# Block two of a transformer kernel: fill matmuls and a paired start at each layer's entry, and one weight panel more ahead in the group norm

## What is computed

```python
h = _rmsnorm(x, norm_g) * (1.0 + scale[:, None, :]) + shift[:, None, :]
proj = h @ w_in
(q, k, v, g_att, qi, ki, wi, z, xbc, dt_raw, gl_att, gl_ssd) = _split_cols(proj, IN_SIZES)
...
y_att = (o_att * jax.nn.silu(g_att)) @ w_branch_a
...
y = y.reshape(B, L, D_SSM) * jax.nn.silu(z.astype(jnp.float32))
y = y.reshape(B, L, N_GROUPS, D_SSM // N_GROUPS)
y = y * lax.rsqrt(jnp.mean(y * y, axis=-1, keepdims=True) + EPS)
y = (y.reshape(B, L, D_SSM) * ssm_norm_g.astype(jnp.float32)).astype(x.dtype)
y_ssd = y @ w_branch_s
merged = jax.nn.sigmoid(gl_att) * y_att + jax.nn.sigmoid(gl_ssd) * y_ssd
return x + gate[:, None, :] * (merged @ w_out)
```

## Time and profile before

| what | us |
|---|---|
| median of 3 runs | 2490.84 (2490.64 to 2492.44) |
| the profiled execution, its time | 2492.25 |
| the profiled execution, its span | 2490.5 |
| TensorE busy in it | 2397.2 |
| VectorE busy | 1421.7 |
| ScalarE busy | 1020.8 |
| POOL busy | 273.9 |
| mean granted TensorE clock, share of full | 0.98 |

### The profile page before, as it was taken

How to read it: one execution, slowest core, us unless ns; L and a number is a source line. 1 busy time by engine, 2 the same in 40 slices (tenths; PEclk the granted TensorE clock), 3 DMA queues, 4 the chain that set the end, 5 groups by cost and what they waited for, 6 DMA issues and landing times.

```text
span 2490.5 us, 31846 instructions
## 1 busy us (share of the span) xinstructions
PE 2397.2 (96%) x11996; PEld 1933.0 (78%) x11996; DVE 1421.7 (57%) x2366; ACT 1020.8 (41%) x1732; POOL 273.9 (11%) x260
## 2 busy tenths in 40 slices
PE   8998899999999999999999989999999899999998
PEld 7876788888887888788888856778788677677886
DVE  3545665655655666566456459947533478665333
ACT  3655564322334444443233334444322344444223
POOL 0000011000000000100000236302000133111001
PEclk9999799999999999999999989999999999999999
DMA  5211002333332111134334212201222221102321
GB/s 193 94 51 43 1 18 93 140 141 127 142 129 87 67 52 60 60 110 152 137 112 159 96 57 68 68 26 43 85 95 94 74 71 65 43 27 76 102 93 51
DMA packets 58038, 211.75 MB, mean 85 GB/s; under 512 B 6432, under 2 KB 6560, under 8 KB 57888
## 3 DMA queue, kind: packets, MB, share of 16 engines
q1 hardware_dynamic: 57456, 208.86, 24.1%
q10 hardware_dynamic: 432, 0.85, 0.1%
HBM read 207.60 MB, written 2.10 MB: 84 GB/s over the span
## 4 chain that ended last, share of the span: by engine, by line
PE 83%; DVE 7%; issue 5%; ACT 4%; POOL 1%; DMA 0%; SPq 0%; ACTq 0%; DVEq 0%; POOLq 0%
PE bank L458 75%; PE last_bank L458 5%; PE bank L468 3%; DVE arena L1105 1%; DVE arena L2190 1%; DVE arena L2192 1%; ACT wparts L545 1%; DVE small L796 1%; ACT arena L784 1%; DVE wparts L549 0%; POOL rstd L604 0%; DVE hT L707 0%; DVE hv L699 0%; DMA ring<-weights_dram 0%; ACT arena L2098 0%
## 5 line engine op out<-in xcount | busy, mean ns | idle before, releaser
L458 PE MATMUL bank<-hT,wparts 128*128 128x512 f32 x5568 | 1353.5, 399 | 16.7 <-DVE hT L707 6.6
L458 PEld LDWEIGHTS bank<-hT,wparts 128*128 128x128 f32 x5568 | 1043.4, 190 | 259.2 <-issue 23.1
L549 DVE TENSOR_TENSOR wparts<-ring,wparts 128x1024 fp32r<-128x1024 f32 x290 | 366.9, 1265 | 433.1 <-ACT wparts L545 432.8
L458 PE MATMUL bank<-arena_r,wparts 128*128 128x512 f32 x2400 | 566.1, 396 | 0.0
L458 PEld LDWEIGHTS bank<-arena_r,wparts 128*128 128x128 f32 x2400 | 450.0, 188 | 108.5 <-DVE arena_r L579 0.3
L545 ACT ACTIVATE wparts<-ring 128x1024 fp32r<-128x1024 f32 x332 | 348.4, 1050 | 163.7 <-PE bank L458 135.7
L784 ACT ACTIVATE arena<-bank,small 128x128 f32<-128x128 f32 (+3 forms) x192 | 101.1, 527 | 142.0 <-DVE small L796 140.5
L468 PE MATMUL bank<-cf_sb,arena 128*128 128x128 f32 (+1 forms) x816 | 134.6, 283 | 17.7 <-DMA cf_sb<-cf_dram 4.7
L458 PE MATMUL last_bank<-arena 128*128 128x64 f32 x992 | 139.6, 279 | 8.0 <-DVE arena L819 3.8
L458 PEld LDWEIGHTS last_bank<-arena 128*128 128x128 f32 x992 | 131.3, 201 | 15.9 <-issue 8.5
L796 DVE TENSOR_REDUCE small<-bank 128x1 f32<-128x128 f32 (+3 forms) x192 | 93.4, 487 | 58.6 <-PE bank L458 56.7
(11 more groups left out here) (273 smaller groups left out, 2113.1 us busy)
## 6 DMA issues: line engine op xcount, KB each, us to landing
ring<-weights_dram SPq DMA_DIRECT2D x388, 512.0 KB, 3.3
arena<-x_dram SPq DMA_DIRECT2D x4, 512.0 KB, 5.7
out_dram<-arena SPq DMA_DIRECT2D x4, 512.0 KB, 4.0
rot<-rot_dram SPq DMA_DIRECT2D x1, 512.0 KB, 10.5
rot<-rot_dram ACTq DMA_DIRECT2D x1, 512.0 KB, 2.9
cf_sb<-cf_dram SPq DMA_DIRECT2D x1, 416.0 KB, 8.8
cb_sb<-cb_dram SPq DMA_DIRECT2D x1, 264.0 KB, 9.8
vecs<-vec_dram ACTq DMA_DIRECT2D x1, 258.5 KB, 5.8
```

Source lines behind the costliest of these rows:

```text
L458: i = pe.matmul(*args, **kw)
L549: eng.tensor_tensor(wparts[:, slot, 1, :, :], ring[:, p % RAW, :, :], wparts[:, slot, 0, :, :].bitcast(F32), ALU.subtract)\
```

## The change

- New `pe_pair`: takes two banks and, for each k, waits for h once and runs the three matmuls of panel one and the three of panel two. `project` uses it for its first two items when `busy` is given; those are qi 0 and qi 1 in both layers. The rope of item 0 is then issued directly behind the pair, and the rope of item 1 after the first 9 matmuls of kki.
- New `pe_busy`: so many bf16 matmuls of 512 columns (identity by a constant) into the bank that was just taken; the real product then overwrites it. 15 ahead of the tokens `xn`, 7 ahead of the spread `L0h`, 9 ahead of the pair in layer 0; 12 ahead of the tokens, 5 ahead of the spread, 12 ahead of the pair in layer 1. Where fills stand, the bank is taken before the wait.
- `AHEAD[4]` is `gls` instead of `gla`.

```diff
+        def pe_pair(pe, keys, rhs, ready, busy=0):
+            taken = [banks.take(pe, key) for key in keys]
+            pe_busy(pe, taken[0], busy)
+            first = tile_no[0]
+            for k in range(KD):
+                pe.wait_ge(*ready(k))
+                for m, (key, bank) in enumerate(zip(keys, taken)):
+                    tile_no[0] = first + KD * m + k
+                    (hi, lo), ends = tile_of(pe)
+                    last = k == KD - 1
+                    mm(pe, bank[:, :], lhsT=hi, rhs=rhs[:, 0, k, :], start=(k == 0), stop=False)
+                    mm(pe, bank[:, :], lhsT=hi, rhs=rhs[:, 1, k, :], start=False, stop=False)
+                    mm(pe, bank[:, :], lhsT=lo, rhs=rhs[:, 0, k, :], start=False, stop=last,
+                       done=key if last else None, ends=ends)
+            for m, key in enumerate(keys):
+                banks.panel_of[key] = first // KD + m
+
+        def pe_busy(pe, bank, n):
+            for _ in range(n):
+                mm(pe, bank[:, :], lhsT=identb, rhs=cstb("cmp")[:, 0:SEQ], start=True, stop=True)
...
-        def pe_by_token(pe, key, sums, weight, last):
+        def pe_by_token(pe, key, sums, weight, last, busy=0):
 
             pe.wait_ge(*pool_made["means"])
-            pe.wait_ge(*pool_made[last])
-            bank = banks.take(pe, (key, "ms"))
+            if busy:
+                bank = banks.take(pe, (key, "ms"))
+                pe_busy(pe, bank, busy)
+                pe.wait_ge(*pool_made[last])
+            else:
+                pe.wait_ge(*pool_made[last])
+                bank = banks.take(pe, (key, "ms"))
...
-        def pe_all_partitions(pe, key, diagonal, pool=ALL_BANKS):
-            pe.wait_ge(*dve_made[key, "diagonal"])
-            bank = banks.take(pe, (key, "rep"), pool)
+        def pe_all_partitions(pe, key, diagonal, pool=ALL_BANKS, busy=0):
+            if busy:
+                bank = banks.take(pe, (key, "rep"), pool)
+                pe_busy(pe, bank, busy)
+                pe.wait_ge(*dve_made[key, "diagonal"])
+            else:
+                pe.wait_ge(*dve_made[key, "diagonal"])
+                bank = banks.take(pe, (key, "rep"), pool)
...
-                    pe_by_token(pe, key, sums, 0, (key, "sum", KD - 1))
-                    pe_all_partitions(pe, key, sums)
+                    pe_by_token(pe, key, sums, 0, (key, "sum", KD - 1), 12)
+                    pe_all_partitions(pe, key, sums, busy=5)
...
-                    linear = pe_linear_steps(pe, it["key"], it["n"], hT, KD, ready if i == 0 else None, pool)
+                    if busy is not None and i < 2:
+                        if i == 0:
+                            pe_pair(pe, [(two["key"], two["n"]) for two in items[:2]], hT, ready, busy)
+                        linear = iter(())
+                    else:
+                        linear = pe_linear_steps(pe, it["key"], it["n"], hT, KD, ready if i == 0 else None, pool)
...
-            pe_by_token(pe, "xn", s1, 0, ("xn", "sum", KD - 1))
+            pe_by_token(pe, "xn", s1, 0, ("xn", "sum", KD - 1), 15)
             pe_by_token(pe, "xs", s2, 0, ("xs", "sum", KD - 1))
-            pe_all_partitions(pe, "L0h", s2)
+            pe_all_partitions(pe, "L0h", s2, busy=7)
             pe_all_partitions(pe, "xn", s1)
...
-            then(project(items, h_at(hk), rtmp, vt, ROPE32))
+            then(project(items, h_at(hk), rtmp, vt, ROPE32, busy=12 if l else 9))
...
-            AHEAD = {0: "ya", 4: "gla"}
+            AHEAD = {0: "ya", 4: "gls"}
```

More of the change, by code:

```diff
@@ L892, in lo_of, with project @@
             return lambda k: dve_made[(key, k), "lo"]
-        def project(items, ready, rtmp, vt, table=None, vt_free=None, pool=ALL_BANKS, norm=None, first=False, summed=False):
+        def project(items, ready, rtmp, vt, table=None, vt_free=None, pool=ALL_BANKS, norm=None, first=False, summed=False, busy=None):
             made = act_made if norm is None else dve_made
```

## The result

The changed kernel takes 2475.07 us (median; 2474.76 to 2478.57), before it was 2491.39 in the same session: ratio 0.9938, 95% interval 0.9926 to 0.9951. That is 16 us, 0.62%. The forecast was 2475.0, with 2470 to 2482 as range. The profiled execution of the changed kernel took 2478.57, its span is 2476.7.

A forecast was written before the change was run, and what follows sets the result against it. TensorE, busy for 96% of the span and holding 83% of the chain that ended last, bounds the kernel. Gains of 5.5 + 4.2 + 2.8 + 1.3 + 2.8 = 16.6 from 2492.25 give 2475.7; forecast 2475.0, range 2470 to 2482.

The forecast's parts named there:

- the 5.5 taken: Layer 0's entry: gain chosen between 3.0 (clock falls) and 6.2 (clock full throughout), near the upper end.
- Price of a fill: All fills: a bf16 matmul of 512 columns takes 0.23 us at full clock, 0.43 at the low clock.
- Layer 0 with the clock full: Layer 0's entry: faster tokens (-1.4), faster spreads (-1.5) and the paired panels gain 6.2 us in all.
- Rival A: The clock falls in layer 0's entry in most executions, which gains 3.0, not 5.5: about 2477.7 us; chance 0.20.
- the spreads keep 1.5: Layer 0's entry if the clock falls: the spreads stay 1.5 us slower, part of why only 3.0 is left.
- Layer 1: Layer 1's entry: fills halve the spread (-1.0) and the pair shortens the projection, -4.2 us, ends 3.2 and 5.0.
- Group norm: Merges: converting the second gls panel early removes TensorE's wait, -2.8 us per layer; layer 0's clock stays up, -1.3 more.
- rival B: Another wait replaces the group norm's, giving back up to 2.3 us in each layer: about 2480 us; chance 0.09.
- Rival C: Both entries: fills overrun their holes and the pair runs at the low clock, slower overall: about 2504 us; chance 0.02.
- Rival D: The pairing buys nothing, TensorE being on VectorE's pace already; the second panel's 5.5 stays: about 2483 us; chance 0.05.
- Sum: Whole kernel: 5.5 + 4.2 + 2.8 + 1.3 + 2.8 = 16.6 us gained, giving 2475.7 from the profiled 2492.25.

The follow-up runs named there:

- double_fills: The changed kernel with every group of fills doubled (30, 14, 18; 24, 10, 24): 2482.74 us, ratio 0.9968 to the kernel before.
- full_again: The changed kernel unaltered, run again in a later session beside variants: 2472.88 us, ratio 0.9926 to the kernel before.
- dve_last_sum: The changed kernel, with VectorE instead of POOL adding the last of eight sums of squares, and shorter fills (12, 5, 9; 9, 5, 12): 2478.22 us, repeated 2474.23.
- fewer_fills: The changed kernel with every group of fills cut by half (8, 4, 5; 6, 3, 6): 2478.75 us, ratio 0.9953 to the kernel before.
- gn_only: The kernel before with only the group norm's key changed (gls for gla), both entries as before: 2485.22 us against 2490.73, ratio 0.998.
- fills_only: The changed kernel without the pair and without the group norm's key, third fills ahead of the first panel: 2486.87 us, ratio 0.9988.

## Why the prediction was right

The time came out at the forecast, and most terms did too. But the forecast assumed that the clock would seldom fall in layer 0's entry, and it fell in three profiles of four; that layer 0 still gained the 5.5 taken is partly luck, as the second and third points show.

- *Price of a fill*, taken as 0.23: 14 and 7 at full clock take 3.19 and 1.67, which is (3.19 - 1.67)/7 = 0.217. In layer 1 of the change 12 and 5 take 2.75 and 1.24, which is 0.216, the price that double_fills is worked out with.
- *Layer 0 with the clock full* (forecast 6.2): 6.65 in full_again. The second tokens end 5.8 us after the last output matmul (7.1 before), -1.3 for -1.4. Eight of them take 1.02 to 1.05 with the clock full; the 0.95 that the prediction reads from the earlier trace rows isn't there. The spreads take 1437.81 to 1439.80, 2.0 for 3.55, -1.6 for -1.5. The first projection matmul comes 11.8 after the output matmul for 14.7, the 2.9 worked out. From the pair's start to the next item 12.2 were worked out (11.0, 0.25, 0.92), and 11.76 to 11.78 measured in layer 0 of the four profiles of full entries. The matmuls are right (11.19 with the drain); the rope was oversized: it starts 0.56 ahead of the next item and not 0.92.
- *Rival A* was right in its premise and wrong in its price, and the forecast the other way round. The fall was priced at 2.5 to 3.2 and costs 1.0. The step that failed in it is "the spreads keep 1.5". In the change the granted clock is low from 1440.95 to 1444.36. The seven fills end just as it comes back, so the spreads run at full clock (1.02), and what remains is mostly the overrun, 0.85 where 1.1 was worked out. With the five fills of dve_last_sum it is low for as long (1440.74 to 1444.15), but the first spread starts in it and takes 2.04. With the four of fewer_fills it is low for twice as long (1437.49 to 1444.31), and the spreads take 2.07 and 1.91. In the profiles with the fall the entry gained 5.6. The term of 5.5 thus holds by two errors that cancel, a fall that was thought unlikely and a price that was about three times too high.
- *Layer 1* (-4.2): 4.75. The first low part of h is ready at 1959.97 and the pair starts at 1960.03, so the fills have no overrun where 0.2 was worked out, and the rope again was 0.36 too long. The granted clock is at 1.00 throughout (1951.2 to 1971.2); in gn_only, with the waits, it is at 0.50 from 1952.5 to 1966.0. Against gn_only's entry it is 5.6.
- *Group norm* (-2.8 each, and -1.3 for the clock): 4.12 and 2.77. The cover worked as laid out: VectorE has 1.22 to spare where 1.0 was worked out. No next wait came; rival B falls.
- *Rival C*: its first step, fills that overrun at the low clock, happened in the three profiles with the fall (0.85 in the change); the low clock did not last into the pair. double_fills has the other half of it, at full clock (1.00 from 1430 to 1460 and from 1950 to 1976): extra fills land on the path for three quarters of their time.
- *Rival D* priced the pairing at 5.5, the whole second panel. It is worth 3.8 in each layer; the prediction's own terms, 6.2 less 2.9, had made it 3.3. Its 2483 follows from neither: 5.5 back in one layer gives 2480.5, in both 2486.
- *Sum*: 16.6 worked out, 17.3 by place in the two profiles; 16.3 by medians. The medians of the change in the other two sessions, 18.4 and 15.7, show how far luck enters the last digit.

## What to carry to other kernels

In this kernel a matmul stream that waited for another engine paid twice, by the wait and by the low clock behind it: in layer 1's entry of gn_only TensorE waits 2.89 us ahead of the tokens, and they take 1.84 us and the spread 2.08, 1.05 and 1.12 in the change. Cheap matmuls (0.217 us each) into a bank that is about to be overwritten removed most of the second cost, where they held the clock and ended before the chain did. Size them from the gap in the timeline: half of them lost the clock, and twice as many cost 9.9 us. And when steps arrive at another engine's pace, let two panels share them: here the pair was worth 2.4 to 3.3 us in the two entries without the full clock, and 3.8 in each with it.

## What had not been expected

*The part that the change leaves alone moves by up to 7.6 us.* The last output matmul of block one ended between 1428.0 (gn_only) and 1435.6 us (the change). The first 60 us of the kernel before, of the change and of full_again, columns as in the earlier trace rows:

```profile
0.00:60.00 60.00, 51.49 (x253) 0.91 0.52 191
```

```profile
0.00:60.00 60.00, 51.59 (x234) 0.86 0.50 184
```

```profile
0.00:60.00 60.00, 50.56 (x269) 0.97 0.57 205
```

In the same 60 us 253, 234 and 269 matmuls are done, at a granted clock of 0.91, 0.86 and 0.97. This work is the same in all kernels, and yet the clock's first fall came at times between 13.1 and 15.4 us; the two profiles with it at 15.4 (fills_only, full_again) reached block two at 1430.1 both. Over the first 1425 us the clock records of the traces have it at 0.50 for 37.5 us in gn_only, 41.0 in full_again, 44.4 in the kernel before and 51.2 in the change, in the order in which block one ended (1428.0, 1430.1, 1432.2, 1435.6). dve_last_sum, with 54.6 us and 1435.5, is the one out of that order, by 0.1. So the traces show that the time of the first fall differs from execution to execution; what sets it they don't show. The 27 executions of the kernel before in one session spread from 2485.9 to 2495.4. Thus differences of 1 to 2 us can't be read from five executions of this kernel each; they can be read from stretches inside a profile.

*A gain can be taken back by the clock alone*, as behind the shorter entries above: 0.9 of 1.0 us, at small matmuls that the edit doesn't touch. It isn't tied to the short entry. The 18 matmuls behind layer 0's small ones take 4.37 us in six of the twelve profiles and 5.55 to 5.99 in the other six. Among these are the kernel before (5.98), gn_only and fills_only, and the change itself has 4.37; this is the 0.8 that it gained between the entries. Behind layer 1's entry it is six of twelve again, in part others. Whether a shorter entry makes the fall more frequent stays open.
